# A state space stage without hi/lo halves: decays from running sums broadcast through DRAM, differences on GpSimd

## The reference

```python
a_cs = cumsum(dt * a)                                   # per head, within the chunk
seg  = exp(where(causal, a_cs[l] - a_cs[s], -inf))      # 16 heads x 128 x 128
cb   = einsum("bclgn,bcsgn->bgcls", cc, bc)
y_diag = einsum("bghcls,bcsghp->bclghp", cb * seg, xc)
states = einsum("bcsgn,bghcs,bcsghp->bcghpn", bc, exp(a_cs[-1] - a_cs), xc)
carry  = exp(a_cs[-1]) * carry + states                 # from chunk to chunk
y_off  = einsum("bclgn,cbghpn,bghcl->bclghp", cc, previous_carry, exp(a_cs))
y = y_diag + y_off + d_skip * xs
```

## Time and profile before

| | us |
|---|---|
| median of 3 runs | 3397.98 (3392.05 to 3400.08) |
| the profiled execution's own time | 3408.66 |
| its span, first to last instruction | 3406.9 |
| TensorE busy | 3176.5 (93%) |
| VectorE busy | 1878.7 (55%) |
| ScalarE busy | 1368.0 (40%) |
| GpSimd busy | 0.2 |

### The profile page before, as it was taken

How to read it: one execution, slowest core, us unless ns; L and a number is a source line. 1 busy time by engine, 2 the same in 40 slices (tenths; PEclk the granted TensorE clock), 3 DMA queues, 4 the chain that set the end, 5 groups by cost and what they waited for, 6 DMA issues and landing times.

```text
span 3406.9 us, 39364 instructions
## 1 busy us (share of the span) xinstructions
PE 3176.5 (93%) x15816; PEld 2571.0 (75%) x15816; DVE 1878.7 (55%) x2435; ACT 1368.0 (40%) x2240; POOL 0.2 (0%) x4
## 2 busy tenths in 40 slices
PE   8999989789999989999999799999999889999987
PEld 6777768577898778888887577677888668877766
DVE  6552678753354344443444535789889543246753
ACT  4321545432253211111113334678878424246741
POOL 0000000000000000000000000000000000000000
PEclk9999977789999989999999899899999989989988
DMA  4113200311311222322221211100011121211031
GB/s 141 44 50 105 67 25 1 112 37 56 90 30 57 72 78 84 90 85 74 81 84 46 90 50 53 41 1 10 10 36 59 62 81 50 78 38 44 11 99 62
DMA packets 228115, 202.84 MB, mean 60 GB/s; under 512 B 8992, under 2 KB 202656, under 8 KB 227424
## 3 DMA queue, kind: packets, MB, share of 16 engines
q1 hardware_dynamic: 224352, 187.49, 17.9%
q10 hardware_dynamic: 3584, 12.85, 1.1%
HBM read 167.54 MB, written 30.41 MB: 58 GB/s over the span
## 4 chain that ended last, share of the span: by engine, by line
PE 85%; DVE 8%; ACT 4%; issue 2%; DMA 1%; SPq 0%; ACTq 0%; DVEq 0%
PE P L298 55%; PE P L267 5%; PE P L2058 5%; PE P L270 3%; PE P L272 2%; PE P L271 2%; PE P L2072 2%; PE P L2071 1%; PE P L2583 1%; PE P L2578 1%; PE P L398 1%; PE P L1346 1%; PE P L2580 1%; PE P L2582 1%; DVE T L1701 1%
## 5 line engine op out<-in xcount | busy, mean ns | idle before, releaser
L254 DVE TENSOR_TENSOR wl<-wf,wh 128x1024 fp32r<-128x1024 f32 (+4 forms) x239 | 251.7, 1053 | 1046.5 <-ACT wh L246 1046.3
L246 ACT ACTIVATE wh<-wf 128x1024 fp32r<-128x1024 f32 (+4 forms) x239 | 220.1, 921 | 1180.1 <-PE P L298 1071.3
L298 PE MATMUL P<-AQ,wh 128*128 128x512 f32 x1920 | 522.7, 394 | 16.5 <-DVE AQ L1314 10.4
L298 PE MATMUL P<-XH,wh 128*128 128x512 f32 (+1 forms) x1376 | 445.7, 406 | 74.7 <-DVE XL L1212 22.9
L298 PEld LDWEIGHTS P<-AQ,wh 128*128 128x128 f32 x1920 | 364.6, 190 | 96.5 <-issue 15.1
L298 PE MATMUL P<-XL,wh 128*128 128x512 f32 (+1 forms) x1376 | 435.8, 399 | 0.0
L298 PE MATMUL P<-XH,wl 128*128 128x512 f32 (+1 forms) x1376 | 435.2, 398 | 0.0
L298 PEld LDWEIGHTS P<-XH,wh 128*128 128x128 f32 (+1 forms) x1376 | 260.2, 192 | 153.9 <-issue 79.8
L298 PEld LDWEIGHTS P<-XL,wh 128*128 128x128 f32 (+1 forms) x1376 | 263.9, 192 | 59.8
L298 PEld LDWEIGHTS P<-XH,wl 128*128 128x128 f32 (+1 forms) x1376 | 263.4, 191 | 59.5
L298 PE MATMUL P<-AQ,wl 128*128 128x512 f32 x960 | 298.0, 392 | 0.0
(11 more groups left out here) (419 smaller groups left out, 5339.6 us busy)
## 6 DMA issues: line engine op xcount, KB each, us to landing
AW<-ada_w SPq DMA_DIRECT2D x48, 512.0 KB, 3.7
wf<-w_gate_up SPq DMA_DIRECT2D x44, 512.0 KB, 4.9
wf<-w_in SPq DMA_DIRECT2D x28, 512.0 KB, 3.8
scratch_g<-T ACTq DMA_DIRECT2D x24, 512.0 KB, 3.3
scratch_h<-H SPq DMA_DIRECT2D x24, 512.0 KB, 5.6
H<-scratch_h SPq DMA_DIRECT2D x24, 512.0 KB, 8.0
wf<-odd_w_in SPq DMA_DIRECT2D x20, 512.0 KB, 3.7
wf<-even_w_in SPq DMA_DIRECT2D x17, 512.0 KB, 3.8
```

The source lines that it names most:

```text
L246: e.activation(self.sb["wh"][i % 2][:, 0:m], self.sb["wf"][i % 2][:, 0:m], ACT.Copy).then_inc(*self.s.w_hi.up(i))
L254: e.tensor_tensor(l, f, h.bitcast(F32), ALU.subtract).then_inc(*self.s.w_lo.up(i))
L298: ins = e.matmul(self.P[slot][0:m, t:t1], w, x[:, k, t:t1], start=first and k == 0, stop=last and k == kb - 1)
```

## The change

No halves in this stage: B and C are fp32 (`BC`), every product is one fp32 matmul, and the `hi`/`lo` steps go. The negated running sums are written to DRAM (`scratch_a`, 64 KB); SP reads each chunk's 16 x 128 values back to all 128 partitions (`RM`, 1 MB in 512-byte pieces, three buffers). GpSimd takes max and difference per head with one `tensor_scalar` of 128x128, and ScalarE makes exp(-x). The causal mask is in `CB`. GpSimd also makes `XD` and scales the state (`STM`). `off` now goes to P2, like `st`. Gates and residual are issued by SP inside the stage. New functions replace `act_moves`, `dve_dt_parts` and `pe_decays`; the sums' write stands at tile 8 of conv.

```diff
@@ sp_conv
+        self.sp_weights(e, self.no["so", 0])
+        e.wait_ge(*self.s.dt.to("rows"))
+        self.sp_rows(e, 0)
+        self.sp_rows(e, 1)
         self.sp_weights(e, self.no["so", 2])
@@ act_dt_parts
+        e.activation(rows, ACS, ACT.Copy, scale=-1.0).then_inc(*self.s.act.up("rows"))
+        e.activation(ea, ACS, ACT.Exp).then_inc(*self.s.act.up("ea"))
+        e.wait_ge(*self.s.act.to("rows"))
+        e.dma_start(self.dr["aT"], rows).then_inc(*self.s.dt.up("rows"))
+    def sp_rows(self, e, n):
+        e.dma_start(self.sb["RM"][n % 3][:, :, :],
+                    self.dr["aT"][:, 128 * n:128 * n + 128].partition_broadcast(128)).then_inc(*self.s.r[n % 3].up(n))
+    def sp_ssd(self, e):
+        e.wait_ge(*s.mm.to(("conv", 11)))
+        self.sp_rows(e, 2)
+        for n in range(3, 8):
+            if n == 4:
+                for j in range(8):
+                    e.dma_start(self.sb["GZ"][:, j, :], self.dr["gT"][:, j, :]).then_inc(*s.gl[j].up("in"))
+            if n == 5:
+                self.sp_reload(e, "back1")
+            e.wait_ge(*s.mm.to(("in", n - 3, 1)))
+            self.sp_rows(e, n)
@@ pe_inside
+            ins = e.matmul(self.P[3][:, hs], self.sb["RM"][c % 3][:, h, :], self.sb["XC"][c % 2][:, hs], start=True,
+                           stop=True)
@@ pe_ssd: the order is tx, tb, cb (n); off, in, st (c); back (c - 1)
             if c > 0:
+                e.wait_ge(*s.dve.to(("st", c - 1)))
                 for g in range(2):
+                    ins = e.matmul(pm[:, gs], BC[:, 2 + g, cs], sb["ST"][:, gs], start=True, stop=True)
             if c >= 0:
+                self.pe_inside(e, c, 0)
                 self.pe_inside(e, c, 1)
             if 0 <= c < 7:
+                e.wait_ge(*s.act.to(("bt", c)))
+                e.wait_ge(*s.pool.to(("xd", c)))
+                if c:
+                    e.wait_ge(*s.dve.to(("yt", c)))
...
@@ act_ssd
+            x = sb["RM"][n % 3][:, 8 * g:8 * g + 8, :]
+            e.wait_ge(*s.pool.to(("seg", n, g)))
+            e.activation(x, x, ACT.Exp, scale=-1.0).then_inc(*s.act.up(("exp", n, g)))
@@ pool_ssd
+        def differences(n):
+            e.wait_ge(*s.r[n % 3].to(n))
+            for h in range(16):
+                x, a = sb["RM"][n % 3][:, h, :], sb["NA"][:, 16 * n + h:16 * n + h + 1]
+                e.tensor_scalar(x, x, a, a, ALU.max, ALU.subtract).then_inc(
+                    *s.pool.up(("seg", n, h // 8) if h % 8 == 7 else None))
+
+        differences(0)
+        for n in range(8):
+            if n < 7:
+                e.wait_ge(*s.dve.to(("xc", n)))
+                if n > 1:
+                    e.wait_ge(*s.mm.to(("st", n - 2)))
+                e.tensor_tensor(self.hd(sb["XD"][n % 2][:, :]), self.hd(sb["XC"][n % 2][:, :]), self.tok(1, n),
+                                ALU.mult).then_inc(*s.pool.up(("xd", n)))
+                differences(n + 1)
+            if 1 < n:
+                cd = sb["CDB"][:, :].rearrange("p (c h) -> p c h", c=8)[:, n - 1, :].unsqueeze(2)
+                e.wait_ge(*s.dve.to(("st", n - 2)))
+                e.tensor_tensor(self.hd(sb["STM"][:, :]), self.hd(sb["ST"][:, :]), cd.to_broadcast([128, 16, 64]),
+                                ALU.mult).then_inc(*s.pool.up(("stm", n - 1)))
@@ dve_ssd: the order is xc, cb (n); yt (c); weigh (n, both groups); y, st (c); back (c - 1)
             if 0 <= c < 7:
+                e.wait_ge(*s.mm.to(("st", c)))
+                if c:
+                    e.wait_ge(*s.pool.to(("stm", c)))
+                    e.tensor_tensor(ST, pm, sb["STM"][:, :], ALU.add).then_inc(*s.dve.up(("st", c)))
...
```

More of the change, by code:

```diff
@@ L857, in act_dt_parts @@
     def act_dt_parts(self, e):
-        w1, w2, w3 = self.sb["dtw"]
-        ACH, ACL, ANH, ANL = self.sb["acs_r"]
+        rows, ea = self.sb["dtw"]
         ACS = self.sb["ACS"][:, :]
[L861 to L891, removed]
+        e.activation(rows, ACS, ACT.Copy, scale=-1.0).then_inc(*self.s.act.up("rows"))
[5 more added lines that the diff above has]
+                    self.dr["aT"][:, 128 * n:128 * n + 128].partition_broadcast(128)).then_inc(*self.s.r[n % 3].up(n))
     def dve_dt_diagonals(self, e):
@@ L930, in tok @@
         return t[:, i, c, :].unsqueeze(2).to_broadcast([128, 16, 64])
[L932 to L943, removed]
+    def sp_ssd(self, e):
+        s = self.s
+        e.wait_ge(*s.mm.to(("conv", 11)))
[8 more added lines that the diff above has]
+            self.sp_rows(e, n)
     def pe_inside(self, e, c, g):
[L946 to L949, removed]
+        e.wait_ge(*self.s.dve.to(("wgh", c, g)))
         for h in range(8 * g, 8 * g + 8):
-            hs, ms = slice(64 * h, 64 * h + 64), slice(128 * (h - 8 * g), 128 * (h - 8 * g) + 128)
-            ins = self.three(e, self.P[3][:, hs], mh[:, ms], ml[:, ms], xh[:, hs], xl[:, hs], True, True)
+            hs = slice(64 * h, 64 * h + 64)
+            ins = e.matmul(self.P[3][:, hs], self.sb["RM"][c % 3][:, h, :], self.sb["XC"][c % 2][:, hs], start=True,
+                           stop=True)
         ins.then_inc(*self.s.mm.up(("in", c, g)))
@@ L959, in pe_back @@
             b = slice(128 * j, 128 * j + 128)
-            ins = self.turn(e, self.P[0][:, b], self.T[2][:, b])
+            ins = self.turn(e, self.P[0][:, b], self.T[2 + c % 2][:, b])
         ins.then_inc(*self.s.mm.up(("back", c)))
     def pe_ssd(self, e):
-        sb = self.sb
+        sb, s = self.sb, self.s
         pt, pb, pm, py = self.P
[L966 to L971, removed]
+        BC, XS = sb["BC"], sb["XS"]
+        e.wait_ge(*s.act.to(("xs", 7)))
+        for slot in range(4):
+            self.pe_place(e, slot)
         for c in range(-1, 8):
@@ L988, in pe_ssd @@
[L988 to L996, removed]
-                for g in range(2):
[L998 to L1006, removed]
@@ new lines, in pe_ssd @@
+                if n:
+                    e.wait_ge(*s.act.to(("bt", n - 1)))
+                    e.wait_ge(*s.dve.to(("cb", n - 1)))
+                for g in range(2):
+                    ins = self.turn(e, pb[:, 128 * g:128 * g + 128], BC[:, g, ns])
+                ins.then_inc(*s.mm.up(("tb", n)))
+                for g in range(2):
+                    ins = e.matmul(pb[:, 512 + 128 * g:640 + 128 * g], BC[:, g, ns], BC[:, 2 + g, ns], start=True,
+                                   stop=True)
@@ L1115, in back @@
+            e.wait_ge(*s.dve.to(("cb", n)))
+            e.tensor_tensor(x, x, cb, ALU.mult).then_inc(*s.dve.up(("wgh", n, g)))
         def back(c):
             x = XS[:, :, 128 * c:128 * c + 128]
-            e.wait_ge(*self.s.mm.to(("back", c)))
-            e.wait_ge(*self.s.act.to(("skip", c)))
-            e.tensor_tensor(x, pt.rearrange("p (j l) -> p j l", j=8), x, ALU.add).then_inc(*self.s.dve.up(("bk", c)))
-        e.wait_ge(*self.s.mm.to(("conv", 11)))
-        e.wait_ge(*self.s.act.to(("xs", 7)))
@@ L1123, in dve_ssd @@
-        e.wait_ge(*self.s.act.to("tokens"))
-        e.wait_ge(*self.s.dt.to(15))
-        e.wait_ge(*self.s.dve.here())
-        e.tensor_copy(sb["RS"][:, 0:1], self.con("eps")).then_inc(*self.s.dve.up("ssd"))
-        heads(0)
+            e.wait_ge(*s.mm.to(("back", c)))
+            e.wait_ge(*s.act.to(("skip", c)))
+            e.tensor_tensor(x, pt.rearrange("p (j l) -> p j l", j=8), x, ALU.add).then_inc(*s.dve.up(("bk", c)))
+        e.wait_ge(*s.act.to("tokens"))
         for c in range(-1, 8):
-            n = c + 1
-            w = n % 2
+            n, YT = c + 1, self.T[2 + c % 2]
@@ L1147, in dve_ssd @@
-                low(("M", n, 0), sb["ML"][0][:, :], self.ew(0), sb["MH"][0][:, :])
+                                ALU.mult).then_inc(*s.dve.up(("cb", n)))
+            if c > 0:
+                e.wait_ge(*s.mm.to(("off", c)))
+                if c > 1:
+                    e.wait_ge(*s.mm.to(("back", c - 2)))
+                e.tensor_tensor(self.hd(YT), self.hd(pm), self.tok(2, c), ALU.mult).then_inc(*s.dve.up(("yt", c)))
+            if n < 8:
+                weigh(n, 0)
+                weigh(n, 1)
@@ L1148, in dve_ssd @@
             if c > 0:
                 back(c - 1)
-                e.wait_ge(*self.s.mm.to(("off", c)))
-                e.tensor_tensor(self.hd(YT), self.hd(pb), self.tok(2, c), ALU.mult).then_inc(*self.s.dve.up(("yt", c)))
-            if n < 8:
-                weigh(n, 1)
-                low(("xd", n), sb["XD"][w][1][:, :], XC, sb["XD"][w][0][:, :])
-            if c > 0:
-                e.wait_ge(*self.s.mm.to(("in", c, 1)))
-                e.wait_ge(*self.s.dve.to(("yt", c)))
-                e.tensor_tensor(YT, py, YT, ALU.add).then_inc(*self.s.dve.up(("y", c)))
@@ L1172, in dve_ssd @@
-            if n < 8:
-                low(("M", n, 1), sb["ML"][1][:, :], self.ew(1), sb["MH"][1][:, :])
-                if n < 7:
-                    e.wait_ge(*self.s.mm.to(("e", n, 1)))
-                    heads(n + 1)
-            if 0 <= c < 7:
```

(6 more changed lines are left out.)

231 lines of the change are left out of this document (82 added, 149 removed).

## The result

The changed kernel takes 3412.83 us (median of 9, 3406.64 to 3415.59), the kernel before 3400.49 in the same runs: ratio 1.0031, 95% interval 1.0018 to 1.0045. The forecast was 3362 us, a gain. The profiled execution took 3410.28 us, its span is 3408.5.

What follows compares the result with a forecast made beforehand. TensorE was taken as the bound, VectorE close behind. Stage 30, gate wait 4.1 and conv's end 1.5 sum to 35.6 us saved from the median 3397.98, giving 3362, range 3335 to 3402.

Steps and rivals of the forecast that it cites:

- GpSimd's small operation: State space stage: each of 16 `tensor_scalar` of 128x128 per chunk on GpSimd would take 0.39 us.
- the ring: Stage loop: from `STM` through state sum, `bk`, transposes and `XC` to `XD`, GpSimd stands still 5.4 us.
- Five rounds: Stage, `XC(2)` to `XC(7)`: 17.7 us each, 88.5 for 99.7 before.
- the 3 for rows: Stage: decay rows queue behind gates and residual, 3 us late in all, between 0 and 10.
- the opening: Stage start, first transpose to `XC(2)`: 19 us at the mixed clock, for 38.5 before.
- conv's end: Before the stage: four moves leave ScalarE's queue ahead of the last tile, so 1.5 us goes.
- slow small operations: Rival, chance 0.17: GpSimd's 16 operations per chunk at 0.87 us give back all 35.6 us; at 1.22, 3428.
- The broadcasts: SP's queue: first two 1 MB row loads ahead of the `so` slabs, 8 to 12 us, cost 0, at worst 5.
- sum of products: TensorE's work per chunk after the change: 19.2 us at the low clock, 14.1 at 0.68.
- TensorE stays at 1.2 GHz: Rival, chance 0.12: in the stage TensorE keeps the low clock, its ring 20.7 us, stage 160 for 167, 3385.
- The held port: Rival, chance 0.13: GpSimd operations and `weigh` exclude each other in full, 6 to 18 us over five rounds, 3374.
- Transfers at the end: Behind the stage: gates and residual loaded inside it, so the 4.1 us wait for the first gate tile goes.

Runs made afterwards that it cites:

- the run with fast broadcasts: Changed kernel with only the running sums stored by chunk, so each partition reads one 8 KB piece; 3405.73 us, 1.0002 to the kernel before.
- the fastest version: Changed kernel with differences moved to VectorE behind `bk` and sums stored by chunk; 3343.80 us, 0.9833 to the kernel before.

## Why the prediction was wrong

**GpSimd's small operation** is the step that failed. I took 0.39 us, ScalarE's time for the same form, between ends of 0.21 and 0.75. It is 0.77 by itself and 0.88 as a mean in the ring, above both ends. The multiply was 1.90 for my 2.44. Five rounds were 88.5 us in the sum, with 3 more for rows, and took 128.5. Of the 37 too many, five rounds of 23.7 for 17.7 are 30, the first round (below) adds 10, and the 3 for rows did not come. Bounds taken from other engines do not bound this one, and the chance of 0.17 was too low for a term on which all depended.

The terms add up: 37 for the rounds, 6.6 for the opening, 4.9 at conv's end, less 5.5 behind `XC(7)`, make 43 us, and the first gate product came at 664.0 where the forecast put it at 621.0. The medians are 51 apart, 12 slower than before for 36 faster; the remaining 8 lie in the spread of single executions.

The rival "slow small operations" had the mechanism. That its break-even of 0.87 lies at the measured 0.88 is in part luck: its round was 25.4, the measured one is 23.7, and the first round makes up the difference.

**The ring** was right in its members and nearly in its price: 5.83 us of GpSimd's idleness for 5.4. Moving `STM` off it gave 31 us over the changed kernel. A measured round of 23.7 is 12.4 for the small operations at 0.77, 3.8 for the multiplies, 5.8 of idleness and 1.7 of waiting beside `weigh`; the forecast had 6.2, 4.9, 5.4 and 1.2.

**The first round** was not in the sum. I let the opening end with `XC(2)` and five equal rounds follow. GpSimd had chunks 0 to 3 to prepare first and caught up at 543.5, so `XC(2)` to `XC(3)` took 33.5 us. The opening itself was 25.6 for 19: in it two `weigh` waited 5.7 us each for exponentials, which waited for GpSimd.

**The broadcasts** were sized by memT's 6.0 us and the slabs' 3.8. Both were wrong neighbours: they landed in 14.7 to 26.9. "Costs 0, at worst 5" at conv's end became 4.9 against the expected gain of 1.5, and GpSimd's start was 12 us later than in the run with fast broadcasts. In the rounds the rows were never late, only because these were long; with the differences on VectorE they cost 4.0 and 2.3 us.

**TensorE** does one round's work in 12.0 us (546.03 to 557.99), at a clock of 0.80 in that stretch. The forecast's 19.2 us at the low clock are 12.0 at 0.80, so its sum of products was right; what was off is the clock, 0.80 for 0.68. The 64-column products stream at 0.11 us a record at the high clock. TensorE never bound, and "TensorE stays at 1.2 GHz" did not happen.

**The held port**, VectorE and GpSimd keeping each other waiting, is real, and it acts in the ring too. The changed kernel's trace, GpSimd's `XD` and four places of `weigh`:

```profile
510.46 1.90 POOL L1041 TENSOR_TENSOR XD<-XC,TOK 128x1024 f32<-128x1024 f32 x1
```
```profile
504.74 1.23 DVE L1060 TENSOR_TENSOR RM<-RM,CB 128x1024 f32<-128x1024 f32 x1 [5.74 <-ACT RM L1000]
511.62 1.84 DVE L1060 TENSOR_TENSOR RM<-RM,CB 128x1024 f32<-128x1024 f32 x1 [5.65 <-ACT RM L1000]
520.66 1.22 DVE L1060 TENSOR_TENSOR RM<-RM,CB 128x1024 f32<-128x1024 f32 x1 [0.97 <-ACT RM L1000]
...
553.00 2.43 DVE L1060 TENSOR_TENSOR RM<-RM,CB 128x1024 f32<-128x1024 f32 x2
```

A `weigh` that meets the multiply `XD` takes 1.84 us for 1.22. One that meets small operations (504.74, 520.66, 553.00) is not lengthened; there it is GpSimd that waits: of the 16 small operations from 551.23 fifteen lasted 0.78 to 0.79 us and one, beside the two `weigh` at 553.00, 2.46. So GpSimd loses 1.7 us a round, for the 1.2 that I charged. Beside conv's end the first 16 cost 1.24 us each. In the fastest version, where GpSimd has only multiplies, two `weigh` cost VectorE up to 2.2 us a round. The Trainium skill ("SBUF — State Buffer", Who interferes with whom) names this contention and says that whichever starts first holds the other up. The traces agree for the multiplies; with the small operations only GpSimd was held up, although they ran back to back and `weigh` started second. The Trainium skill's ratio of 1.96 for GpSimd against VectorE ("GPSIMD Engine Reference", Performance versus the Vector engine) is, for these multiplies, 1.90 to 1.22, 1.6.

**Transfers at the end:** the 4.1 us wait went, as said. From `XC(7)` to the first gate product it was 21.0 for a forecast of 26.5.

## What to carry to other kernels

An engine that is new in a loop has prices of its own, for an instruction, for an element and for the kind of operand. When no row shows them, let the rival with the high price carry the weight, or measure one instruction first. Wide operations save the fixed part, which here was by estimate a fifth of the cost. Draw the ring before summing rounds, with the work that piles up before the first one, and take off it whatever another idle engine can do. Look at the contiguous piece that each partition reads: storing 64 KB in the order of its readers made eight transfers three times as fast. But ask also what queues behind a transfer: putting two slabs ahead of the slow broadcasts was worth as much.

## What the runs showed of the hardware

- A DMA that broadcasts 1 MB to 128 partitions took 16.0 us (median) in 512-byte pieces and 4.7 in pieces of 8 KB, from a buffer of the same size. Slabs in 512-byte pieces from large matrices land in 3.8 us for half the bytes, so the small piece alone does not explain the whole; what a shared source adds was not parted from it.
- GpSimd's `tensor_scalar` of 128x128 took 0.49 us with a constant, 0.58 with one per-partition operand and 0.77 with two and a second step, from start to start and with nothing beside it; VectorE's with two took 0.26. Of 128x1024, GpSimd's maximum with a constant took 2.76 and its multiply, with one operand more, 1.90.
- The longest small operation on GpSimd, 2.85 us for 0.79, was not the first (1.05 us) but one at 480.83, beside a conv tap and a weight split of VectorE. In the ring one per round lasted 2.5 to 2.7 beside two `weigh`. In the fastest version it is the other way round too: VectorE's 16 small operations took 4.85 us for 4.18 where they began during a multiply of GpSimd.
- An fp32 product of 64 columns costs 0.22 us at the high clock (two records), as much as two fp32r products of the same form (0.11 each), so that one fp32 product is cheaper than the three fp32r products of the halves. With 512 columns it is the other way: about 0.89 us (four records of the changed kernel in 1.78, from 555.17) against three of 0.23.
